# A weight ring of ten slots in laps over eight experts, rows gathered in three bf16 parts, and an unweighted scatter, in a two-layer mixture-of-experts decoder

## The reference

```python
def expert_block(args):
    xb, e = args
    return (jax.nn.silu(xb @ w_gate[e]) * (xb @ w_up[e])) @ w_down[e]
...
y_buf = lax.map(expert_block, (x_buf, blk_e)).reshape(p, d)
y_buf = y_buf * w_buf[:, None].astype(y_buf.dtype)
out = jax.ops.segment_sum(y_buf, tok_buf, num_segments=n)
```

## Time and profile before

| What | us |
|---|---|
| Median of 3 runs | 1234.75 (1227.23 to 1238.0) |
| Profiled execution | 1236.96 |
| Its span, first to last instruction | 1235.1 |
| TensorE busy | 1162.1 (94%) |
| VectorE busy | 423.1 (34%) |
| ScalarE busy | 189.9 (15%) |
| Moved | 439.30 MB, mean 356 GB/s |

### The profile page before, as it was taken

One profiled execution on the slowest core, in us unless ns is written; L12 is line 12 of the kernel. 1 busy time (PEld: TensorE's weight loads), 2 busy tenths in 40 slices (PEclk: granted clock), 3 DMA queues, 4 the chain that ended last, 5 costly groups with the idle time before them and its releaser, 6 DMA issues.

```text
span 1235.1 us, 13944 instructions
## 1 busy us (share of the span) xinstructions
PE 1162.1 (94%) x5646; PEld 552.8 (45%) x5646; DVE 423.1 (34%) x748; ACT 189.9 (15%) x374; POOL 8.1 (1%) x36
## 2 busy tenths in 40 slices
PE   6997999999999999999989989899999999999988
PEld 5984453333333333333379855433333333333333
DVE  3746243322222232222266572532223223222223
ACT  3417210000000000000044161100001000000000
POOL 2000000000000000000000000000000000000000
PEclk9999999999999999999989999899999999999999
DMA  9665069999999999999984350799999999999996
GB/s 359 182 260 205 1 248 429 420 419 430 428 429 427 431 426 431 426 431 426 416 323 189 137 205 10 330 428 415 416 428 429 427 430 427 431 426 430 426 430 267
DMA packets 53904, 439.30 MB, mean 356 GB/s; under 512 B 14192, under 2 KB 14192, under 8 KB 29296
## 3 DMA queue, kind: packets, MB, share of 16 engines
q1 hardware_dynamic: 53872, 438.85, 85.8%
HBM read 437.79 MB, written 1.05 MB: 355 GB/s over the span
## 4 chain that ended last, share of the span: by engine, by line
PE 75%; DMA 18%; DVE 4%; ACT 2%; issue 1%; DVEq 0%; SPq 0%; ACTq 0%
PE bank L1493 42%; DMA ring<-in_moe_w_up 11%; PE bank L1382 8%; DMA ring<-in_moe_w_gate 6%; PE bank L1422 4%; PE bank L1471 4%; PE bank L1505 4%; PE bank L1377 3%; PE bank L1481 1%; PE bank L1536 1%; PE bank L1299 1%; PE bank L1210 1%; PE bank L1529 1%; PE bank L1392 1%; PE bank L1250 1%
## 5 line engine op out<-in xcount | busy, mean ns | idle before, releaser
L1493 PE MATMUL bank<-ring,qkT 128*64 128x512 f32 x2944 | 655.0, 597 | 27.9 <-DMA ring<-in_moe_w_gate 15.4
L1493 PEld LDWEIGHTS bank<-ring,qkT 128*64 128x64 f32 x2944 | 204.8, 137 | 453.8 <-issue 407.7
L1174 DVE TENSOR_SCALAR qkT<-qkT 128x512 f32<-128x512 f32 x32 | 13.7, 428 | 486.4 <-ACT qkT L748 486.4
L1176 DVE RECIPROCAL qkT<-qkT 128x512 f32<-128x512 f32 x32 | 107.3, 3353 | 1.1
L1505 PE MATMUL bank<-qkT 64*128 64x512 f32 x256 | 63.6, 615 | 5.6 <-ACT qkT L753 5.6
L1181 DVE TENSOR_TENSOR qkT<-bank,qkT 128x512 f32<-128x512 f32 x32 | 22.1, 692 | 131.7 <-PE bank L1493 131.7
L753 ACT ACTIVATE qkT<-bank 128x512 f32<-128x512 f32 x32 | 19.1, 597 | 304.3 <-PE bank L1493 304.3
L1422 PE MATMUL bank<-ring,hn 128*128 128x512 f32 x128 | 55.7, 593 | 1.2 <-ACT hn L663 0.7
L748 ACT ACTIVATE qkT<-bank 128x512 f32<-128x512 f32 x32 | 19.1, 598 | 243.2 <-PE bank L1493 243.2
L944 DVE TENSOR_TENSOR w_low<-ring,w_high 128x2048 fp32r<-128x2048 f32 x22 | 49.4, 2286 | 11.6 <-ACT w_high L596 11.6
L1471 PE MATMUL bank<-fn_high,take 128*128 128x512 f32 x136 | 47.8, 434 | 0.0
(11 more groups left out here) (214 smaller groups left out, 872.3 us busy)
## 6 DMA issues: line engine op xcount, KB each, us to landing
ring<-in_moe_w_gate SPq DMA_DIRECT2D x64, 2048.0 KB, 22.1
ring<-in_moe_w_down SPq DMA_DIRECT2D x64, 2048.0 KB, 24.9
ring<-in_moe_w_up SPq DMA_DIRECT2D x56, 2048.0 KB, 24.4
ring_spare<-in_moe_w_up SPq DMA_DIRECT2D x8, 2048.0 KB, 26.5
ring<-in_ab_w_in SPq DMA_DIRECT2D x12, 1024.0 KB, 14.1
ring<-in_c_w_in SPq DMA_DIRECT2D x12, 1024.0 KB, 14.7
ring<-in_ab_w_out SPq DMA_DIRECT2D x2, 2048.0 KB, 15.2
ring<-in_c_w_out SPq DMA_DIRECT2D x2, 2048.0 KB, 15.2
```

Of the source, the lines that this page charges most:

```text
L1176: nc.vector.reciprocal(sig, sig).then_inc(s.gate_step, 1)
L1493: last = mm(b[SLOTS * half:SLOTS * (half + 1), :], left(h, k), expert_rhs(slot, k, half), start=(h == 0 and k == 0), stop=(h == 1 and k == ...
```

## The change

The ring gets nine slots and the spare one, ten in all. PLACES lays the 48 units of eight experts (OCTET) in laps of 10, 10, 10, 9 and 9; the loops over experts run over eight turns instead of four. Slot 8 is loaded (unit 2 of expert 1) right behind the output weights, without a wait, and the spare slot gets unit 3. The room comes from laying cum and cum_neg over bias_a and from a smaller scratch for dynamic DMAs.

The normed rows are held in three bf16 parts: ScalarE rounds the row (high), VectorE computes the rest in fp32 (low), ScalarE rounds that (mid), VectorE subtracts (lowest). take is bf16 and 64 wide, without zeros beside it. The gather has 12 matmuls of 64 columns, in pairs on both halves of the array.

The scatter uses an unweighted giveT (0 or 1, fp32r) and two parts of the weighted y: VectorE takes each slot's weight as a maximum over tokens and makes giveT by comparison; ScalarE writes y_high = y * w rounded to fp32r, VectorE y_low = y * w - y_high. 8 fp32r matmuls per turn, and the scatter waits for both parts.

```diff
-RING = 8
+RING = 9
 SPARE = RING
-QUAD = 4
-QUAD_UNITS = QUAD * UNITS
-PLACES = [(SPARE, 0) if i == RING else ((i - (i > RING)) % RING, (i - (i > RING)) // RING)
-          for i in range(QUAD_UNITS)]
+OCTET = 8
+OCTET_UNITS = OCTET * UNITS
+LAPS = (10, 10, 10, 9, 9)
+SLOT_OF_UNIT = [slot for slots in LAPS for slot in range(slots)]
+PLACES = [(slot, SLOT_OF_UNIT[:i].count(slot)) for i, slot in enumerate(SLOT_OF_UNIT)]
...
                 load_wout(layer)
+                load_unit(layer, RING - 1, RING - 1 - UNITS, 1)
                 sp.wait_ge(s.out_psum, 4 * layer + 4)
-                for slot in range(UNITS, RING):
+                for slot in range(UNITS, RING - 1):
                     load_unit(layer, slot, slot - UNITS, 1)
...
-                act.wait_ge(rt_shift, layer + 1)
-                act.activation(rt[:, 2], rt[:, 1], ACT.Exp).then_inc(rt_exp, 1)
+                    if t == 1:
+                        act.wait_ge(rt_shift, layer + 1)
+                        act.activation(rt[:, 2], rt[:, 1], ACT.Exp).then_inc(rt_exp, 1)
+                    act.wait_ge(rest_ready, NT * layer + t + 1)
+                    act.activation(fn_parts[1][:, t, :], rest, ACT.Copy).then_inc(rows_mid, 1)
...
-                        act.wait_ge(s.giveT_psum, now)
-                        act.activation(giveT[k % 2], GATE[:, 0:T], ACT.Copy).then_inc(s.giveT_ready, 1)
-                        act.wait_ge(*used(s, quad, k, 5))
-                        act.activation(y_sb, Y[:, :], ACT.Copy).then_inc(s.y_ready, 1)
+                        act.wait_ge(s.giveT_ready, now)
+                        act.wait_ge(*used(s, octet, k, 5))
+                        act.activation(y_high[:, :], Y[:, :], ACT.Copy,
+                                       scale=w_slot[:, k % 2:k % 2 + 1]).then_inc(s.y_high, 1)
...
-                    stt(fn_low[:, t, :], x_sb[:, t, :], root_y[:, t:t + 1],
-                        fn_high[:, t, :].bitcast(F32), ALU.mult, ALU.subtract).then_inc(rows_low, 1)
+                    stt(rest, x_sb[:, t, :], root_y[:, t:t + 1], fn_parts[0][:, t, :], ALU.mult,
+                        ALU.subtract).then_inc(rest_ready, 1)
+
+                def lowest(t):
+                    dve.wait_ge(rest_ready, NT * layer + t + 1)
+                    dve.wait_ge(rows_mid, NT * layer + t + 1)
+                    tt(fn_parts[2][:, t, :], rest, fn_parts[1][:, t, :], ALU.subtract
+                       ).then_inc(rows_low, 1)
...
                 low(0)
-                for t in range(NT):
-                    for side in (0, 2):
-                        ts(take[:, t, SLOTS * side:SLOTS * (side + 1)], slot_id[:, 0, :], -1.0, None,
-                           ALU.is_equal)
                 add(2)
                 leave_transposed(layer, 1, gain_ffn, (0, 1), 0)
+                lowest(0)
...
                 last.then_inc(chosen, 1)
+                low(1)
 
                 dve.wait_ge(rank_psum, layer + 1)
...
                         make_take(layer, 0)
-                        low(1)
+                        lowest(1)
...
-                        make_give(layer, turns(quad, k + 1))
+                        nc.vector.tensor_reduce(w_slot[:, k % 2:k % 2 + 1], GATE[:, 0:T], AX_X, ALU.max)
+                        ts(giveT[k % 2][:, :], GATE[:, 0:T], 0.0, None, ALU.is_gt
+                           ).then_inc(s.giveT_ready, 1)
+                        make_give(layer, turns(octet, k + 1))
+                        dve.wait_ge(s.y_high, turns(octet, k + 1))
+                        stt(y_low[:, :], Y[:, :], w_slot[:, k % 2:k % 2 + 1],
+                            y_high[:, :].bitcast(F32), ALU.mult, ALU.subtract).then_inc(s.y_low, 1)
...
-                    for t in range(NT):
-                        for i, part in enumerate((fn_high, fn_low)):
+                    for i, (rows_made, part) in enumerate(zip((rows_high, rows_mid, rows_low), fn_parts)):
+                        pe.wait_ge(rows_made, NT * (layer + 1))
+                        for t in range(NT):
...
-                                side = SLOTS * (1 - h)
-                                last = mm(MISC[:, :], take[:, t, side:side + P],
+                                last = mm(MISC[SLOTS * h:SLOTS * (h + 1), :], take[:, t, :],
...
                     pe.wait_ge(s.giveT_ready, count)
+                    pe.wait_ge(s.y_high, count)
+                    pe.wait_ge(s.y_low, count)
+                    for y in (y_high, y_low):
+                        for t in range(NT):
+                            for half in range(2):
+                                r = slice(SLOTS * half, SLOTS * (half + 1))
+                                last = mm(ACC[2 * t + half][:, :], giveT[k % 2][r, P * t:P * (t + 1)],
+                                          y[r, :], start=False, stop=False, skip_group_check=True)
...
-    nc = bacc.Bacc("TRN2", target_bir_lowering=False, num_devices=1)
+    nc = bacc.Bacc("TRN2", target_bir_lowering=False, num_devices=1, dynamic_dma_scratch_size=1024)
```

More of the change, by code:

```diff
@@ L364, in place, with turns, used @@
             return PLACES[UNITS * k + u]
-        def turns(quad, k):
-            return quad * QUAD + k
-        def used(s, quad, k, u):
+        def turns(octet, k):
+            return octet * OCTET + k
+        def used(s, octet, k, u):
             slot, lap = place(k, u)
-            return s.unit_used[slot], quad * USES[slot] + (lap + 1)
+            return s.unit_used[slot], octet * USES[slot] + (lap + 1)
         def spread_by(layer, j):
@@ L847, in mixed_and_normed @@
                 norm(1)
-                return low
+                return low, lowest
             def make_tables():
@@ L977, in first_of, with route @@
                 own(tt(out_ap, d, spread(rt[:, 5, :, 0:1], [P, NT, 4]), ALU.is_equal))
-            def route(layer, low):
+            def route(layer, low, lowest):
                 s = layers[layer]
@@ L1169, in _ @@
-                with dve.Fori(0, last_quad + 1) as quad:
-                    for k in range(QUAD):
-                        make_take(layer, turns(quad, k + 1))
-                        dve.wait_ge(s.gate_exp, turns(quad, k + 1))
+                last_octet = dve.value_load(last_octets[0:1, layer:layer + 1],
+                                          min_val=N_EXPERTS // OCTET - 1,
+                                          max_val=ROUNDS * N_EXPERTS // OCTET - 1)
+                with dve.Fori(0, last_octet + 1) as octet:
+                    for k in range(OCTET):
+                        make_take(layer, turns(octet, k + 1))
+                        dve.wait_ge(s.gate_exp, turns(octet, k + 1))
@@ L1482, in tokens_out, with two_halves @@
                     last.then_inc(s.xt_psum, 1)
-                def two_halves(b, left, quad, turn, units):
+                def two_halves(b, left, octet, turn, units):
                     for h, u in enumerate(units):
                         slot, lap = place(turn, u)
-                        pe.wait_ge(s.unit_loaded[slot], quad * (USES[slot] * 16)
+                        pe.wait_ge(s.unit_loaded[slot], octet * (USES[slot] * 16)
                                    + ((WIN if slot < UNITS else 0) + 16 * (lap + 1)))
@@ L1498, in scatter @@
                 def scatter(count, k):
-                    pe.wait_ge(s.y_ready, count)
                     pe.wait_ge(s.giveT_ready, count)
-                    for t in range(NT):
-                        for half in range(2):
-                            r = slice(SLOTS * half, SLOTS * (half + 1))
-                            last = mm(ACC[2 * t + half][:, :], giveT[k % 2][r, P * t:P * (t + 1)],
-                                      y_sb[r, :], start=False, stop=False, skip_group_check=True)
-                            last.then_inc(s.scattered, 1)
@@ L1509, in _ @@
-                gather(1, first=True)
+                    pe.wait_ge(s.y_high, count)
[6 more added lines that the diff above has]
+                                          y[r, :], start=False, stop=False, skip_group_check=True)
+                                if y is y_low:
+                                    last.then_inc(s.scattered, 1)
@@ L1510, in _ @@
+                gather(1)
                 tokens_out(1)
                 pe.wait_ge(slots_ready, layer + 1)
-                last_quad = pe.value_load(last_quads[0:1, layer:layer + 1],
-                                          min_val=N_EXPERTS // QUAD - 1,
-                                          max_val=ROUNDS * N_EXPERTS // QUAD - 1)
-                with pe.Fori(0, last_quad + 1) as quad:
-                    for k in range(QUAD):
-                        now, after = turns(quad, k + 1), turns(quad, k + 2)
+                last_octet = pe.value_load(last_octets[0:1, layer:layer + 1],
+                                          min_val=N_EXPERTS // OCTET - 1,
+                                          max_val=ROUNDS * N_EXPERTS // OCTET - 1)
@@ L1518, in _ @@
+                with pe.Fori(0, last_octet + 1) as octet:
```

(6 more changed lines are left out.)

123 lines of the change are left out of this document (64 added, 59 removed).

## The result

The changed kernel takes 1226.26 us in the median of 20 runs, the kernel before 1234.33 in 20: a ratio of 0.9938 [0.9927, 0.9949], 8.1 us less. The profiled execution took 1226.79 us (span 1225.1) against 1236.96: 10.2 us less. The forecast was 1222, and its range of 1214 to 1231 holds the result. It is within the 1% that counted as no change, with a sign that 20 runs settle; the range is wide enough to hold rival (a) too, so the time alone doesn't tell whose mechanism it was. One of the 20 took 4693.55 us; the ratio leaves it out.

The account below looks back on a forecast made before the run. The prediction took the DMA stream of expert weights as the bound. Its terms, -5.8 us in layer 0 and -7.9 in layer 1, sum to -13.7, giving 1223.3 or 1221.1; it forecast 1222 us (chance 0.54), range 1214 to 1231.

Parts of the forecast that it names:

- rival (a): Only the slot counts: slowest engine never ran dry, scatter runs serially, start late in both layers; 1228 us, chance 0.28.
- The stream is the bound: In the experts, loading weights takes 29.4 us per expert, TensorE 26.9 before and 25.4 after, so loading decides.
- One slot, -4.9 per layer: Slot 8, loaded in attention's idle slice, leaves one unit less behind the experts' start: -4.90 us per layer.
- Dry points, -1.3 and -2.0: Early in the experts the load queue runs nearly empty; laps of ten end that: -1.3 us layer 0, -2.0 layer 1.
- The larger loop body: Experts' loops of eight turns instead of four: claimed to cost nothing that the trace shows.
- Gather and scatter: Per expert, 1.4 and 1.0 us by overlapping pairs; only the scatter before the last down product counts, -0.9 us per layer.
- The end of the layer: Behind the last down product, y_low comes before the scatter without cover: +0.8 us per layer.
- The start: The first gather of the experts needs all three parts: +0.5 us in layer 0, -0.9 in layer 1.
- (b): The clock falls in TensorE's waits for DMA during the experts: about 1260 us, chance 0.06.
- (c): Layer 1's first units run at full clock and the dry points give their upper bound: 1219 us, chance 0.12.
- What would show it: Signs include the last expert's second half of up (unit 93) starting at 596.3 and 1200.3 us, and 425 GB/s or more.

Follow-up runs that it names:

- slots_short: Kernel before with ten slots, early load of slot 8 and the 24-unit slot pattern, loops of four, old gather, scatter and start: 1220.80 us, 0.9892.
- ten_short: Changed kernel with loops of four experts instead of eight, ten slots in a 24-unit pattern, loads in the order slots come free: 1219.79 us, 0.9882.
- late_slot: Changed kernel with slot 8 loaded behind the output product together with the other three units, not in the idle slice: 1226.56 us, 0.9939.
- oct_only: Kernel before with loops over eight experts instead of four, its old slots, gather and scatter kept: 1236.42 us, 1.0031.
- short_code2: ten_short with 240 one-column memsets on GpSimd per gather, for which nobody waits: 1252.81 us, 1.0162.
- parts_only: Changed kernel with the old eight slots and spare, old pattern and loops of four; new gather, scatter and start kept: 1230.00 us, 0.9959.
- short_code: ten_short with 256 no-ops on GpSimd after each gather: 1220.29 us, 0.9889.

## Why the prediction was right, and where it was wrong

The forecast's -13.7 us was right for nearly all the steps that it summed, and wrong by one step that it priced at nothing. That the measured 8.1 us still lie in the range owes to its width, not to that step.

- **The stream is the bound.** Right. TensorE needs 24.7 us per expert (25.4 forecast), the stream 29.4; 47 us of busy time went, and slots_short, which keeps the old gather and scatter, is within 1.0 us of ten_short.
- **One slot, -4.9 per layer.** Right: landing 11 of layer 0 (counted from 0) comes 22.10 us after the first product before and 18.86 after, of which 1.69 is the clock, so 4.9 earlier. The place was wrong: late_slot, without the load in the idle slice, has a stretch longer by 0.9 us over both layers and a time longer by 0.3 us, so the slice brings little of it. Nor do the laps of ten matter: ten_short hasn't got them and is faster.
- **Dry points, -1.3 and -2.0.** Confirmed by the windows (422 to 428, 419 to 428 GB/s) and a little larger: the dry points took 1.7 and 2.3 us before, and ten_short's lateness is 1.5 and 2.3 us under that of before. The fit of the Trainium skill that the prediction set beside them (DMA: Bandwidth & Descriptors, "Anatomy of one DMA") would have made it up to 4.0 us per layer; it is given there for transfers issued by GpSimd, and these are issued by SP.
- **The larger loop body, "cost nothing that the trace shows".** This is the step that failed: about +2.4 us per layer. The evidence given for it, no gap at the end of a pass, was about the loop of four, whose code stayed in place, and a gap of TensorE isn't even the cost. Change and ten_short differ by 4.7 us of lateness and by 6.5 us of time (the other 1.8 us aren't accounted for); oct_only has the cost alone, +3.2 us.
- **Gather and scatter.** 1.30 and 1.12 us, forecast 1.4 and 1.0. Pairs on two column halves and on two row halves do overlap.
- **The end of the layer.** y_high, y_low and the scatter take 2.59 us from ScalarE's start to the first copy of ACC (616.23 - 613.64) against 1.81 in the earlier trace rows: +0.8, as forecast. The tail as a whole came out at +0.15 in layer 0 instead of -0.1. In layer 1 it is +0.58, with a last unit that landed 0.4 us late.
- **The start.** Layer 1 gained 0.95 us between the ranks' matmuls and the first product (7.85 to 6.90), forecast 0.9. Layer 0 lost nothing, forecast +0.5: the parts took what was forecast (1.06 and 1.22 us), but low began at 169.08, half a us earlier than assumed.
- **Rivals.** (a), 1228, came nearest in time but by the wrong mechanism: the dry points went, the scatter runs in pairs, the start is early. (b) didn't come: 1.00 at 89% busy; behind the start of the experts the clock fell only where TensorE had stood for 5.6 us, to 0.57 from 380 to 385 us. (c) came in layer 1 and was given back in layer 0.
- **What would show it.** Unit 93 was to start at 596.3 and 1200.3. It came at 600.08 and 1203.28. In layer 0 the 3.8 us are 1.7 of clock and the 2.6 lost in the stream, less 0.6 of the start. The GB/s line couldn't show it: 2.4 us of 400 is 0.6%, under 3 GB/s, as much as the slices scatter.

## What to carry to other kernels

When a loop's body grows, read the instruction queues' lines on the page before and after: a body that no longer stays in place is fetched on every pass, over the engines that carry the weights. Under a full stream each such packet sets one engine back; it costs time when that engine is the slowest, and it costs all of it when the packets always hit the same engine. A prefetch gains by depth only what the stream would otherwise stand still; look at where it stands, not at where there is room. Two changes that remove the same idle time don't add: measure each alone before summing them.

## What the hardware showed that I had not expected

- A loop of four experts was fetched on its first pass (packets at 209, 234 and 260 us in the kernel before). Its later passes in layer 0 had no packet and no gap, and in layer 1 one packet, at 1110 us. A loop of eight was fetched throughout, a packet of 16 KB per expert, and TensorE stood 5.6 us at the jump back (4.8 and 10.5 in oct_only).
- The Trainium skill (Runtime: NRT & Kernel Launch, "Instruction fetch mechanics") gives TensorE 128 KiB for code and says that a taken branch stalls for a fetch when its target isn't in the two pages held. The trace agrees with the size and with the stall: the ten packets of layer 0's second pass are 160 KB, and TensorE stands at the jump to it; a loop of four is half of that, and fits. That only two pages of 16 KiB are held doesn't fit a loop of four, some 80 KB, that jumps back without a fetch or a stand.
- A packet of 16 KB takes about 1.07 us on a DMA engine and, with the slower weight packet behind it, sets it back by 1.55 us. In layer 0 of the kernel after there are 14 more of them than in ten_short (17 against 3), and the lateness is 2.9 us larger. A packet of 8 KB on GpSimd's queue takes 0.31 us and sets its engine back by 0.65. In short_code2 28 of them, always on the same engine, came with a lateness of 17.7 us.
- A unit's landing follows the slowest of its engines. The Trainium skill (DMA: Bandwidth & Descriptors, "Why a DMA increments its semaphore by 16 and not by 1") describes the engines as finishing independently, each with a count of its own. The trace agrees: behind each engine's eight packets of a unit stands a write of 4 bytes of its own, and at the end of short_code2's layer 1 one engine writes its last 16 us behind the others.
- The first 32 records of a layer's experts took 7.09 or 8.78 us in the profiled executions. The longer time came in layer 1 of the kernel before and in layer 0 of the kernel after, parts_only and short_code (8.75). What decides it is open.
